# RWKV scan of a hybrid block: joint score products, decay sums made in the preparation, half masks, the merge's tiles spread

## The reference

```
def step(s, inp):
    w_t, k_t, v_t, kk_t, a_t = inp[:5]
    sa = einsum('bhvk,bhk->bhv', s, kk_t)
    s = (s * w_t[:, :, None, :] - sa[..., None] * (kk_t * a_t)[:, :, None, :]
         + v_t[..., None] * k_t[:, :, None, :])
    return s, einsum('bhvk,bhk->bhv', s, inp[5])      # output for the latent tokens only
```

## Time and profile before

| | us |
|---|---|
| three runs | 2241.96, 2240.7, 2236.75 |
| median | 2240.7 |
| the profiled execution | 2244.75 |
| its span, first to last instruction | 2243.0 |
| the preparation, from VectorE's first instruction to the scan's first | 822.7 to 973.9 |
| the scan, to the merge's first load | 973.9 to 1277.4 |

### The profile page before, as it was taken

How to read it: one execution, slowest core, us unless ns; L and a number is a source line. 1 busy time by engine, 2 the same in 40 slices (tenths; PEclk the granted TensorE clock), 3 DMA queues, 4 the chain that set the end, 5 groups by cost and what they waited for, 6 DMA issues and landing times. The chain is left out here.

```text
span 2243.0 us, 38706 instructions
## 1 busy us (share of the span) xinstructions
PE 2044.1 (91%) x16787; PEld 1683.7 (75%) x16787; DVE 1366.9 (61%) x1287; ACT 786.2 (35%) x858; POOL 275.6 (12%) x135
## 2 busy tenths in 40 slices
PE   7679999999899989966677799989999999999997
PEld 3258888888678876656666688778888888888886
DVE  3465666665438547758888678366565656554444
ACT  1231112113062225524433365344343434333333
POOL 0242213123104214301000020000000000000000
PEclk9589999999899999988999899999999999999998
DMA  9989888886264368977444287535555555555552
GB/s 327 349 273 335 309 310 301 310 316 193 90 170 106 85 186 262 302 194 189 86 88 88 52 205 269 204 120 188 187 187 187 187 188 188 185 206 188 191 199 98
DMA packets 406153, 454.18 MB, mean 202 GB/s; under 512 B 107551, under 2 KB 356751, under 8 KB 388735
## 3 DMA queue, kind: packets, MB, share of 16 engines
q1 hardware_dynamic: 398400, 441.04, 62.0%
q10 hardware_dynamic: 7614, 11.10, 1.3%
HBM read 413.89 MB, written 38.22 MB: 202 GB/s over the span
## 5 line engine op out<-in xcount | busy, mean ns | idle before, releaser
L215 DVE TENSOR_TENSOR f_w_lo<-t_w_raw,f_w_hi 128x2048 fp32r<-128x2048 f32 x132 | 302.2, 2290 | 308.1 <-ACT f_w_hi L209 308.1
L270 PE MATMUL pf<-h,f_w_hi 128*128 128x512 f32 x1320 | 463.9, 395 | 0.0
L209 ACT ACTIVATE f_w_hi<-t_w_raw 128x2048 fp32r<-128x2048 f32 x132 | 253.2, 1918 | 446.8 <-PE pf L270 283.6
L269 PE MATMUL pf<-h,f_w_lo 128*128 128x256 f32 x1320 | 367.4, 278 | 0.3 <-DVE h L2603 0.3
L270 PEld LDWEIGHTS pf<-h,f_w_hi 128*128 128x128 f32 x1320 | 247.6, 188 | 54.3
L269 PEld LDWEIGHTS pf<-h,f_w_lo 128*128 128x128 f32 x1320 | 248.3, 188 | 4.6 <-DVE h L2603 0.6
L209 ACT ACTIVATE p_w_hi<-h_w_raw 128x2048 fp32r<-128x2048 f32 (+1 forms) x52 | 96.4, 1901 | 340.6 <-DVE stage L726 252.2
L261 PE MATMUL p_in<-h,p_w_lo 128*128 128x512 f32 (+1 forms) x512 | 199.3, 389 | 0.0
L259 PE MATMUL p_in<-h,p_w_hi 128*128 128x512 f32 (+1 forms) x512 | 199.3, 389 | 0.0
L260 PE MATMUL p_in<-h,p_w_hi 128*128 128x512 f32 (+1 forms) x512 | 199.3, 389 | 0.0
L2799 PE MATMUL d_out<-f_w_hi,hid 128*128 128x512 f32 x704 | 178.7, 394 | 6.2 <-DVE f_w_lo L215 6.2
(11 more groups left out here) (417 smaller groups left out, 3362.9 us busy)
## 6 DMA issues: line engine op xcount, KB each, us to landing
h_of_x<-in_ada_w SPq DMA_DIRECT2D x64, 1024.0 KB, 5.1
h_w_raw<-in_w_in SPq DMA_DIRECT2D x51, 1024.0 KB, 7.5
t_w_raw<-in_ffn_w_gate SPq DMA_DIRECT2D x44, 1024.0 KB, 5.1
t_w_raw<-in_ffn_w_up SPq DMA_DIRECT2D x44, 1024.0 KB, 5.1
t_w_raw<-in_ffn_w_down SPq DMA_DIRECT2D x44, 1024.0 KB, 4.9
h_w_raw<-in_ada_w SPq DMA_DIRECT2D x32, 1024.0 KB, 8.8
gate_w<-in_w_in SPq DMA_DIRECT2D x32, 1024.0 KB, 6.2
t_w_raw<-in_w_out SPq DMA_DIRECT2D x16, 1024.0 KB, 5.7
```

Of the source, the lines that this page charges most:

```text
L209: act.activation(self.hi[:, m % self.S, 0:w], self.raw[:, s, 0:w], ACT.Copy)\
L215: eng.tensor_tensor(self.lo[:, m % self.S, 0:w], self.raw[:, s, 0:w], b32(self.hi[:, m % self.S, 0:w]), ALU.subtract)\
L269: pe.matmul(hi, wl, x[:, 0, k, :], start=False, stop=False)
L270: return pe.matmul(both, wh, x[:, :, k, :], start=False, stop=last)
```

## The change

It has five parts. (1) The sums of the decays: VectorE makes them in the preparation by a scan over the sigmoids, in place of GpSimd's multiply; the scan stage loads sums, its `b` and its scan instruction go, and the constant goes into the scale of ScalarE's exponentials. (2) For latent chunks one group of products of 128 columns takes the place of the groups of `scores1` and `scores3`; keys are now the weights, so `first` holds the transpose and the masks of the levels are those of the other direction. (3) From the second chunk on the mask of a level is multiplied over half the columns only, with one `step` buffer per level, whose other half keeps what the first chunk wrote. (4) The two products of a state are issued as two groups, with a wait between them; `output` is cut in two steps that follow each other. (5) The merge's first four tiles are issued one per half chunk, from (2, 1) to (4, 0), ahead of `rc`.

```diff
                     for d in range(2):
-                        pool.wait_ge(s_sg, 4 * j + 2 * d + 1)
-
-                        pool.tensor_scalar(dr[:, b, d, 0, :], sg[:, b, 0, d, :], -DECAY_TOP, None, ALU.mult)\
-                            .then_inc(s_lw, 1)
                         pool.wait_ge(s_sg, 4 * j + 2 * d + 2)
...
+                dve.memset(keep[:], 1.0).then_inc(s_keep, 1)
+                dve.wait_ge(s_keep, 1)
+                dve.memset(keep[:].rearrange("p (u c) -> p u c", c=C)[:, :, 0:1], 0.0).then_inc(s_keep, 1)
...
                         dve.tensor_tensor(dr[:, b, d, 2, :], u[:, b, d, :], kmix[:, b, :], ALU.mult).then_inc(s_kd, 1)
+                    for d in range(2):
+                        rev = slice(None, None, -1 if d else 1)
+                        dve.wait_ge(s_sg, 4 * j + 2 * d + 1)
+                        dve.tensor_tensor_scan(out=dr[:, b, d, 0, :][:, rev], data0=keep[:], data1=sg[:, b, 0, d, :][:, rev],
+                                               initial=0.0, op0=ALU.mult, op1=ALU.add).then_inc(s_lw, 1)
...
-        step = pair_of("step", [U8, C])
+        step = pair_of("step", [GROW, U8, C])
...
+        def joining(t, d, l):
+            return t.rearrange("p u (n a w) -> p u n a w", a=2, w=1 << l)[:, :, :, d, :]
...
                 go("output", last)
+                go("output2", last)
                 go("prepare3", now)
                 go("state", last)
+                go("state2", last)
...
-                        for n in ("q1", "b", "s2tr"):
+                        for n in ("q1", "e_end", "s2tr"):
...
-                        raw.prefetch(sp, *first_merge(A))
+                    n = 2 * (c - 2) + d - 1
+                    if 0 <= n < RAW:
+                        sources, shape = first_merge(A)
+                        sp.dma_start(raw.slots[:, n].rearrange("p (k n) -> p k n", k=shape[0]), sources[n])\
+                          .then_inc(raw.landed[n], 16)
...
-                def prepare(c, d):
-                    rev = slice(None, None, -1 if d else 1)
-                    dve.wait_ge(sm("in", d), c * 16 + 16)
-                    if c:
-                        dve.wait_ge(sm("e_end", d), c)
-                    dve.tensor_tensor_scan(out=flat(b[d])[:, rev], data0=keep[:],
-                                           data1=ldr[d][:, 0].rearrange("p u c -> p (u c)")[:, rev], initial=0.0,
-                                           op0=ALU.mult, op1=ALU.add).then_inc(sm("b", d), 1)
...
-                    dve.tensor_tensor(quads(step[d][:]), quads(turned[d][:]), mask(LEVEL + l, d), ALU.mult)\
-                       .then_inc(sm("step", d), 1)
+                    if c == 0:
+                        dve.tensor_tensor(quads(step[d][:, l]), quads(turned[d][:]), mask(LEVEL + l, 1 - d), ALU.mult)\
+                           .then_inc(sm("step", d), 1)
+                    else:
+                        joined = masks[:, 1 - d, LEVEL + l, :].unsqueeze(1).broadcast_to([P, U8, C])
+                        dve.tensor_tensor(joining(step[d][:, l], d, l), joining(turned[d][:], d, l), joining(joined, d, l),
+                                          ALU.mult).then_inc(sm("step", d), 1)
...
-                    act.wait_ge(sm("b", d), c + 1)
+                    act.wait_ge(sm("in", d), c * 16 + 16)
                     if c:
                         act.wait_ge(sm("s12", d), c)
-                    act.activation(es[d][:], b[d][:], ACT.Exp, bias=refs[:, 1:2], scale=-1.0).then_inc(sm("es", d), 1)
+                    act.activation(es[d][:], ldr[d][:, 0], ACT.Exp, bias=refs[:, 1:2], scale=DECAY_TOP).then_inc(sm("es", d), 1)
...
+                    n = 2 if latent(c) else 1
+                    if latent(c):
+                        pe.wait_ge(sm("q2", d), c - 3)
                     for j, h in UNITS:
-                        last = pe.matmul(by_token(pb[d], j, h), feat(q12[d][:, :, 0, :], j, h), feat(ldr[d][:, 1], j, h),
-                                         start=True, stop=True)
+                        last = pe.matmul(by_token_pair(pb[d], j, h, n), feat(ldr[d][:, 1], j, h),
+                                         q12[d][HEAD[h], j, 0:n, :].rearrange("p q c -> p (q c)"), start=True, stop=True)
...
-                def scores3(c, d):
-                    if latent(c):
-                        pe.wait_ge(sm("first", d), c + 1)
-                        for j, h in UNITS:
-                            last = pe.matmul(by_token(pb[d], j, h), feat(ldr[d][:, 1], j, h), feat(q12[d][:, :, 1, :], j, h),
-                                             start=True, stop=True)
-                        last.then_inc(sm("r1s", d), 1)
...
                     pe.wait_ge(sm("uc", d), c + 1)
+                    pe.wait_ge(sm("s2t", d), c + 1)
+                    for j, h in UNITS:
+                        last = pe.matmul(by_feature(pa[d], j, h, 1), flip(s2t[d], j, h), flip(vt[d], j, h), start=j < 2,
+                                         stop=False, skip_group_check=True)
+                    last.then_inc(sm("st_own", d), 1)
+
+                def state2(c, d):
+                    if c == LAST:
+                        return
+                    pe.wait_ge(sm("uc", d), c + 1)
                     pe.wait_ge(sm("s1t", d), c + 1)
-                    pe.wait_ge(sm("s2t", d), c + 1)
-                    for four in FOURS:
-                        for j, h in four:
-                            pe.matmul(by_feature(pa[d], j, h, 1), flip(s2t[d], j, h), flip(vt[d], j, h), start=True, stop=False)
-                        for j, h in four:
-                            last = pe.matmul(by_feature(pa[d], j, h, 1), flip(s1t[d], j, h), tok(u[d], j, h), start=False, stop=True)
+                    pe.wait_ge(sm("st_own", d), c + 1)
+                    for j, h in UNITS:
+                        last = pe.matmul(by_feature(pa[d], j, h, 1), flip(s1t[d], j, h), tok(u[d], j, h), start=False, stop=True,
+                                         skip_group_check=True)
```

More of the change, by code:

```diff
@@ L979, in phase_rwkv_pre @@
         post = alloc(st, "post", [P, 2, 2, SEQ])
+        keep = alloc(st, "keep", [P, TOK])
         pz = [psum(st, f"pz{n}", TOK) for n in range(4)]
@@ L1484, in scores1 @@
                     dve.wait_ge(sm("n", d), c + 1)
-                    dve.copy_predicated(quads(first[d][:]), mask(LOWER, d).bitcast(mybir.dt.uint32), narrow(pb[d]))\
+                    dve.copy_predicated(first[d][:], masks[:, 1 - d, LOWER, :].unsqueeze(1).broadcast_to([P, U8, C])
+                                        .bitcast(mybir.dt.uint32), paired(pb[d])[:, :, 0, :])\
                        .then_inc(sm("first", d), 1)
@@ L1496, in scores3 @@
                     if latent(c):
[L1497 to L1498 removed]
+                        dve.wait_ge(sm("n", d), c + 1)
+                        dve.tensor_tensor(r1[d][:], paired(pb[d])[:, :, 1, :],
+                                          masks[:, d, INCL, :].unsqueeze(1).broadcast_to([P, U8, C]), ALU.mult)\
                            .then_inc(sm("r1", d), 1)
                 def close(c, d):
[L1502 removed]
+                    low, high = (0, 32) if d else (32, 0)
                     dve.wait_ge(sm("grown", d), c * GROW + GROW)
@@ L1539, in output @@
                     dve.tensor_tensor(by_parity(yat), by_parity(yat), narrow(pb[d]), ALU.add).then_inc(sm("ysum", d), 1)
-                run(dict(prepare=prepare, prepare1=prepare1, prepare2=prepare2, prepare3=prepare3, stage=stage, scores1=scores1, scores2=scores2, scores3=scores3,
+                run(dict(prepare1=prepare1, prepare2=prepare2, prepare3=prepare3, stage=stage, scores1=scores1, scores2=scores2, scores3=scores3,
                          close=close, open=open_, halve=halve, state=state, output=output))
@@ L1558, in forward @@
                         act.wait_ge(sm("q2", d), c - 4)
-                    act.activation(decays(d, 0), b[d][:], ACT.Exp, bias=refs[:, 0:1]).then_inc(sm("e2", d), 1)
+                    act.activation(decays(d, 0), ldr[d][:, 0], ACT.Exp, bias=refs[:, 0:1], scale=-DECAY_TOP).then_inc(sm("e2", d), 1)
                 def ends(c, d):
@@ L1564, in ends @@
                         act.wait_ge(sm("S", d), c)
-                    act.activation(e_end[d][:].unsqueeze(2), b[d][:, :, last:last + 1], ACT.Exp).then_inc(sm("e_end", d), 1)
+                    act.activation(e_end[d][:].unsqueeze(2), ldr[d][:, 0, :, last:last + 1], ACT.Exp, scale=-DECAY_TOP).then_inc(sm("e_end", d), 1)
                     if (c, d) == (0, 0):
@@ L1710, in grow @@
                     for j, h in UNITS:
-                        last = pe.matmul(placed(l)(level(d, l), j, h), of(step[d], j, h), of(src[d], j, h),
+                        last = pe.matmul(placed(l)(level(d, l), j, h), of(step[d][:, l], j, h), of(src[d], j, h),
                                          start=True, stop=True)
@@ L1719, in inverse @@
                     for j, h in UNITS:
```

(5 more changed lines are left out.)

25 lines of the change are left out of this document (9 added, 16 removed).

## The result

| | before | after |
|---|---|---|
| median, us | 2239.7 (20 runs) | 2255.05 (20 runs, 2234.46 to 2274.29) |
| ratio of the two | | 1.0059, 95% interval 1.0039 to 1.0079 |
| the profiled execution, its span | 2244.75, 2243.0 | 2269.71, 2267.9 |
| ahead of the preparation | 822.7 | 819.8 |
| the preparation | 151.1 | 181.3 |

The forecast was 2235.4 with a range of 2220 to 2249: wrong, in sign and in range. The executions of the changed kernel lie in two groups of ten: 2234 to 2251 (median 2243.3) and 2259 to 2274 (median 2265.7); those of the kernel before stay within 6 us of their median. The profiled execution belongs to the long group, so its 30 us in the preparation are what the long ones pay.

What follows compares the result with a forecast made beforehand. Bounds: touching TensorE and VectorE chains in the preparation; nearly full VectorE, with waits for TensorE and its pauses, in the scan. Terms 8.5 - 1.2 - 2.0 - 3.2 - 7.0 - 0.4 = -5.3 us: 2240.7 to 2235.4, range 2220 to 2249.

Steps and rivals of the forecast that it cites:

- The pair of the preparation: Preparation: two added VectorE scans, less the wait for `u`, lengthen each head pair by 1.15 us; +8.5 us in all.
- Rival C: Preparation: new scans and GpSimd's neighbour sums lock each other out; 8 to 16 us more, 2243 to 2251; chance 0.12.
- The scan, -13.8 us: Scan stage, all its terms: start -1.2, context slots -2.0, GLA split slot -3.2, latent slots -7.0, tail -0.4.
- The start: Start of the scan stage: the removed VectorE scan was on the path there; -1.2 us.
- the context slots: Five context slots of the scan stage: VectorE's lateness of some 0.4 us behind the second growth goes; -2.0 us.
- the slot with the split of the GLA output: Scan slot where GpSimd splits the GLA output: the scan held 5.54 us goes; -3.2 us (0 to -4.3).
- Seven latent slots: Latent slots of the scan: VectorE loses scan and half masks, TensorE's pauses take some back; -7.0 us (-3 to -12).
- rival B: Scan: TensorE's pauses eat the gain, the stage gives 4 us; total 2245 (2241 to 2247); chance 0.22.
- The end: Tail of the scan, where VectorE already waits for each growth: 0.09 us gained a level; -0.4 us.
- Rival A: Scan: VectorE's lost work counts for more than half; total taken as 2225 us; chance 0.15.
- Part 4 and 5: State products in two groups: between nothing and 0.3 us, taken 0.2; merge's tiles: 0 to -1.5, taken 0.
- The joint score products: Latent slots: 128-column groups of 1.10 us replace 64x64 ones; TensorE gains 0.2 us, some 6% fewer instructions.

Runs made afterwards that it cites:

- neighbours_behind_ks: Changed kernel with GpSimd's neighbour sums of pair j+2 made to wait until `ks` of pair j is done; 2241.60 us, ratio 1.0012.
- full_masks: scans_first with the masks of the levels over all columns again, in the changed kernel's buffers; 2236.40 us, ratio 0.9976.
- joint_state_tiles: Changed kernel without parts 1 and 3: sums made in the scan stage, full masks in one buffer; 2240.97 us, ratio 1.0000.
- gates_ahead: Kernel before, with 15 instead of 10 of a pair's 20 gate products ahead of `pss` and 5 behind, no scan added; 2245.35 us, ratio 1.0031.
- late_neighbours: Changed kernel with GpSimd's neighbour sums of pair j+2 made to wait until both new scans of pair j are done; 2249.29 us, ratio 1.0030.
- short_output: gates_fill without two of the three product groups of a latent half chunk's output, so `y` is incomplete; 2229.97 us, ratio 0.9948 (8.8 under gates_fill).
- gates_fill: Changed kernel with 15 gate products of a pair behind `pss` and 5 ahead, in place of 10 and 10; 2238.76 us, ratio 0.9990.
- scans_first_only: Changed kernel with the two new scans ahead of the products `dr[2]`, gate products still 10 and 10; 2247.01 us, ratio 1.0070.
- scans_first: Changed kernel with the two new scans ahead of `dr[2]`, and 15 gate products behind `pss`, 5 ahead; 2236.98 us, ratio 0.9984.

## Why the prediction was wrong

**The pair of the preparation, +8.5 us.** The sizes of its operations were right: 1.28 us for both products, 2.33 for the scans, an undisturbed pair of 15.2 us against 15.4 forecast. 8 x 0.8 = 6.4 us, and `neighbours_behind_ks`, whose pairs are all of that kind, has a preparation of 154.6 us. The step that failed was to let the new wait of TensorE count as itself: "it is idle for all of it", 8 x 1.15 = 9.2. The wait is 0.75 us where nothing disturbs it and 1.90 to 2.40 us in the six pairs with neighbour sums, and behind those the products run at 1.2 GHz in place of 2.4 for a while: 17.80 us a pair in place of 14.45. The pair then takes 18 to 20 us. No rival had the clock in it, though the earlier trace rows showed 1.00 there with an engine that never paused, which was the thing the change was about to end.

**Rival C, chance 0.12, had the right lock and about the right price for it, and not the clock.** The sums hold the scans (3.97 us in place of 2.33) or `ks` (2.34 for both in place of 0.88), as it said, 1.2 to 1.6 us a pair in six pairs. That alone is 9 us, within its 8 to 16. Of the 30 us of a long execution some 5 are the longer undisturbed pairs, 9 the lock and 18 the clock; 2 us come back ahead of the first `nrm`. The forecast left the lock out of its sum because the sums start "0.4 to 1.3 us behind where the scans will end". Two things were wrong in that. `ks` follows the scans and takes 0.9 us itself, so that sums which miss the scans fall on it, as in the pair of 888.64. And the distance was read at full clock: in a long execution the sums start 1.4 to 3.7 us behind `nrm`, 4.8 to 8.0 in the same pairs before (the second to the sixth).

**The scan, -13.8 us.** It gave 4.0 us in the profiled execution, and 1.0 to 8.1 in the eight profiles of kernels that have all its parts (4.9 on average, against the one profile of before). Taken apart, as averages of these eight:

- The start -2.4 us (forecast -1.2), from 30.7 to 28.3.
- The stretch from the first to the eighth `close`: +3.3 us against the kernel before, where the context slots were to give 2.0 and the slot with the split of the GLA output 3.2. That slot did fall, from 22.1 to 16.7 to 19.8 us: the lock on the scan is gone, and a mask takes 3.13 us there in the changed kernel, as the forecast had it. But the slot ahead of it grew from 14.4 to 16.2 to 18.5, by the new pause of 2.4 to 2.7 us. Pauses were counted for latent slots alone; this was the failed step here. It isn't the whole: the three slots behind the split are 4.5 us longer together, and the pauses in them only by some 2; the rest is open.
- Seven latent slots -3.9 us, that is 0.56 each, where eight were to give 7.0, 0.9 each. The masks take 0.42 us as forecast, against 0.60 for ScalarE's copy from the same moment. The view of L1713 still names `step` in 61 of its waits and `grown` in 15, where `grown` was forecast; a mask that is 0.27 us shorter without effect in `full_masks` speaks for the forecast's reason, the view doesn't. VectorE's lost work became its wait behind TensorE: rival B in its mechanism (0.22), and the stage's 4.9 us are near the 4 that it gave.
- The end -2.0 us (forecast -0.4).

**Rival A** is refuted for the masks by `full_masks`: 16.8 us of VectorE's work cost no time. **Part 4 and 5** were costed at 0.2 us and nothing; `joint_state_tiles` agrees (2240.97). **The joint score products** take 1.10 and 1.08 us for a group of 128 columns at full clock, as forecast.

Put together for a short execution: 2239.7 + 3.5 to 6.4 - 4.9 is 2238 to 2241, and the short group has 2243.3; for a long one 2239.7 + 30.2 - 4.9 is 2265, and the long group has 2265.7. The median lies between them, because half the executions are of either kind. What decides which kind an execution becomes was not tried; with the lock taken away only the short kind is left in twelve executions.

The best kernel that ran is `full_masks` (scans ahead of `dr[2]`, 15 gate products behind `pss`, full masks): 0.24% faster than before (0.10 to 0.37%).

## What to carry to other kernels

Where TensorE runs without a gap at full clock, an edit that opens a recurring wait isn't priced by the wait's length: look what it does at the two levels of the clock, and give TensorE something to do there (five gate products moved in each pair gained 16 us here, with the lock gone by the same edit). When an instruction moves on VectorE, look again at the GpSimd instructions that it can lock with, against it and against all that follows it, at their new time and not at the old one. And VectorE's busy share of 80% in the scan was no bound: 36 us of its work could go for 4 us, because each wait for TensorE took the place of the work removed.

## What the runs showed of the hardware

- The wait behind which TensorE's clock falls is short and not sharp. In the profiled executions every pair with a wait for `ks` of up to 0.88 us, and no wait for a load, kept 1.00. Of ten pairs with 1.22 to 1.52 us seven kept it and three fell to 0.90 (1.22 in `gates_ahead`, 1.41 and 1.42 in `late_neighbours`). Of 32 pairs with 1.78 to 3.69 us 29 fell to 0.79 to 0.91; three single ones of 1.86 to 2.09 us, in `short_output`, `gates_fill` and `scans_first_only`, kept 1.00.
- The lock between VectorE and GpSimd comes and goes with the time at which a load lands, so the same list of instructions has pairs with and without it. In the profile of the changed kernel it costs TensorE 9.0 us of waiting, and the low clock behind these waits 18.3 us more.
- GpSimd's `u` (one SBUF tensor and per-partition columns) is also held by VectorE's scan: both directions take 3.91 us beside it in `scans_first`, 0.77 us each in the changed kernel, where no scan runs then.
- TensorE's pauses without a releaser, 32 to 42 us of a scan of some 300 (0.9 us or longer each), stand at the same products in kernels that share the list, beside a count of one 16 KB piece of code for each 126 to 128 records of products.
